# The first MLP matrix in seven block products instead of eight (Strassen), in a two-layer hybrid transformer step

## The reference

```python
def channel_mlp(x, shift, scale, gate, p):
    h = rms_norm(x, p['norm2']) * (1 + scale) + shift
    z = jax.nn.relu(h @ p['mlp_w1'])          # 1024 -> 4096
    return x + gate * ((z * z) @ p['mlp_w2'])  # 4096 -> 1024
```

## Time and profile before

| | |
|---|---|
| median of 3 runs | 1724.19 us (1720.06 to 1725.21) |
| profiled execution, its own time | 1722.82 us |
| its span in the profile | 1720.9 us |
| mean granted PE clock | 0.977 of 2.4 GHz |
| DMA | 160.14 MB, mean 93 GB/s |

### The profile page before, as it was taken

One profiled execution on the slowest core, in us unless ns is written; L12 is line 12 of the kernel. 1 busy time (PEld: TensorE's weight loads), 2 busy tenths in 40 slices (PEclk: granted clock), 3 DMA queues, 4 the chain that ended last, 5 costly groups with the idle time before them and its releaser, 6 DMA issues.

```text
span 1720.9 us, 28384 instructions
## 1 busy us (share of the span) xinstructions
PE 1599.7 (93%) x11714; PEld 1487.7 (86%) x11714; DVE 939.8 (55%) x1493; ACT 658.7 (38%) x1041; POOL 135.4 (8%) x99
## 2 busy tenths in 40 slices
PE   6878997899999999999987789888999999999998
PEld 4756894589999999999976569756999999999998
DVE  4554438846556554655565433596656545554553
ACT  4555434743322322233154463366443322332221
POOL 0003004400000000000000120253000000000000
PEclk9989998999999999999999899989999999999999
DMA  9620544212222222224534206441222222222311
GB/s 315 217 86 1 97 120 133 83 50 74 74 74 74 74 74 74 74 74 145 165 108 150 73 5 141 128 130 30 76 72 74 74 74 81 67 74 74 98 50 62
DMA packets 150855, 160.14 MB, mean 93 GB/s; under 512 B 16390, under 2 KB 132808, under 8 KB 150728
## 3 DMA queue, kind: packets, MB, share of 16 engines
q1 hardware_dynamic: 150024, 158.13, 30.3%
q10 hardware_dynamic: 576, 0.16, 0.0%
q0 software_dynamic: 128, 0.05, 0.0%
HBM read 153.41 MB, written 4.65 MB: 92 GB/s over the span
## 4 chain that ended last, share of the span: by engine, by line
PE 77%; DVE 10%; ACT 7%; issue 3%; SPq 1%; DMA 1%; ACTq 0%; DVEq 0%
PE ps L1591 33%; PE ps L1973 27%; PE ps L1730 10%; DVE extrema L1342 1%; PE ps L1754 1%; PE ps L1571 1%; ACT pt_c L783 1%; DVE extrema L1325 1%; PE ps L1807 1%; PE ps L1617 1%; SPq L606 1%; PE ps L1702 1%; PE ps L1785 1%; ACT pr_c L957 1%; DMA ada_room<-in_w_ada 1%
## 5 line engine op out<-in xcount | busy, mean ns | idle before, releaser
L1384 DVE SCALAR_TENSOR_TENSOR xT<-ps,mod,xT 128x128 f32<-128x128 f32 (+2 forms) x432 | 190.1, 440 | 198.0 <-PE ps L1591 186.1
L783 ACT ACTIVATE w_hi<-w_raw 128x2048 fp32r<-128x2048 f32 (+1 forms) x90 | 169.9, 1887 | 335.2 <-PE ps L1591 327.2
L1148 DVE TENSOR_TENSOR w_lo<-w_raw,w_hi 128x2048 fp32r<-128x2048 f32 (+1 forms) x90 | 203.1, 2257 | 142.6 <-ACT w_hi L783 141.2
L1973 PE MATMUL ps<-xa_hi,w_hi 128*128 128x320 f32 (+1 forms) x1024 | 236.2, 312 | 0.0
L1973 PE MATMUL ps<-xa_lo,w_hi 128*128 128x320 f32 (+1 forms) x1024 | 235.2, 311 | 0.0
L1973 PE MATMUL ps<-xa_hi,w_lo 128*128 128x320 f32 (+1 forms) x1024 | 235.2, 311 | 0.0
L1591 PE MATMUL ps<-z_hi,w_hi 128*128 128x320 f32 x1024 | 234.1, 310 | 0.9 <-DVE xT L1384 0.9
L1591 PE MATMUL ps<-z_lo,w_hi 128*128 128x320 f32 x1024 | 233.4, 309 | 0.0
L1591 PE MATMUL ps<-z_hi,w_lo 128*128 128x320 f32 x1024 | 233.3, 309 | 0.0
L1120 ACT ACTIVATE z_relu<-z_relu,sink_shift 128x128 f32<-128x128 f32 (+1 forms) x128 | 72.3, 564 | 307.4 <-DVE z_relu L1491 305.3
L1973 PEld LDWEIGHTS ps<-xa_hi,w_hi 128*128 128x128 f32 x1024 | 173.5, 189 | 0.3
(11 more groups left out here) (249 smaller groups left out, 2372.5 us busy)
## 6 DMA issues: line engine op xcount, KB each, us to landing
w_raw<-in_mlp_w SPq DMA_DIRECT2D x64, 1024.0 KB, 5.4
ada_own<-in_w_ada SPq DMA_DIRECT2D x54, 512.0 KB, 4.5
w_raw<-in_w_in SPq DMA_DIRECT2D x14, 1024.0 KB, 8.5
ada_mix<-in_w_ada SPq DMA_DIRECT2D x21, 512.0 KB, 7.6
ada_room<-in_w_ada SPq DMA_DIRECT2D x15, 512.0 KB, 9.7
w_raw<-in_w_out SPq DMA_DIRECT2D x8, 768.0 KB, 5.3
ada_first<-in_w_ada SPq DMA_DIRECT2D x6, 512.0 KB, 9.3
x_in<-in_x_sample SPq DMA_DIRECT2D x1, 2048.0 KB, 8.9
```

The source lines that it names most:

```text
L783: do(nc.scalar.activation(out, in_, ACT.Copy), sem)
L1148: do(V.tensor_tensor(w_lo[:, n % 2, 0:w], w_raw[:, n % 2, 0:w], f32(w_hi[:, n % 2, 0:w]), ALU.subtract), w_lo_ready)
L1384: do(V.scalar_tensor_tensor(dst, src, gate[:, m:m + 1], dst, ALU.mult, ALU.add), sem if last else None)
L1973: last = M.matmul(bank(b + a_, s1 - s0), w[r][:, k, c:c + P], x[:, k, s0:s1], start=k == 0 and q == 0, stop=k == KC - 1 and q == 2)
```

## The change

The w1 unit is now computed by Strassen's scheme. Its matrix is cut in two rows (hidden channels 0 to 127 and 128 to 255) by two columns (even and odd input chunks), and the input in even or odd chunks (b11 and b12, b21 and b22: first and second half of the tokens). Seven products of 4 k x 3 = 12 matmuls, each 322 columns wide, take the place of eight: 84 matmuls. Needed for that:

- Four sums of weight quarters, s1 to s4, per w1 unit (`sum_quarters`, DVE, 512 columns each), and four combinations of input halves, t1 to t4, made once a layer (`combine_halves`, DVE). The input now has seven parts of 4 x 322 columns, each with a hi half (ACT) and a lo half (DVE).
- Each w1 unit is split in seven blocks of 512 columns (11, s2, s1, s3, 12, 22, s4), each w2 unit in four; w_hi and w_lo are a ring of eight blocks. A block is split when the block eight places earlier has been multiplied.
- The products are put together from PSUM: two pairs of products add up in a bank (b11 x 11 stays in bank 0, is copied to `us[0]` by ACT, and 12 x b21 is added in the bank), the rest DVE adds in `take_u`, `take_22`, `take_11`, `take_21`, `take_12`.
- z is scaled in `z_raw`; ACT does relu in two segments, squares to z_hi and squares in place; DVE subtracts (`low_z`).
- The order of units alternates: w1, w1, w1, w2, w1, w2, ... (three w2 at the end).
- The adaLN loads of the next layer that went out before and after the last w1 unit all go out after it, since their places are now used by the MLP.

The diff, cut to its core:

```diff
         for g in range(GROUPS):
-            if g + 1 < GROUPS:
-                out += [(l, "w1", g + 1, j) for j in range(2)]
-            out += [(l, "w2", g, j) for j in range(2)]
+            for j in range(2):
+                out += [(l, "w1", g + 1, j)] * (g + 1 < GROUPS) + [(l, "w2", g, j)]
...
+W1_ORDER = ("11", "s2", "s1", "s3", "12", "22", "s4")
+W1_ORDER_FIRST = ("11", "22", "12", "s2", "s1", "s3", "s4")
+X_LO_ORDER = ("b11", "b21", "t4", "t2", "t1", "t3", "b22")
+XW = NTOK // 2 + 2
...
# SP
+                    sp.wait_ge(prod_done, 7 * W1_PER_LAYER * (l + 1))
+                    sp.wait_ge(u_read, 6 * W1_PER_LAYER * (l + 1))
+                    load_adas(48 * (l + 1), range(over + ROOM // 2))
                     load_adas(48 * (l + 1), range(over + ROOM // 2, over + ROOM))
...
# ACT, start of the MLP
+                for j in range(4):
+                    if j < 3:
+                        split_hi(U + 10 + j)
+                    else:
+                        for b in range(3):
+                            split_hi_block(first, b)
+                    for c in (2 * j, 2 * j + 1):
+                        act.wait_ge(m_dve, acc_ix.last_reader(acc_ix.at[(l, "wo", c)])[1])
+                        scale_halves(l, c)
+                        square_x(2 * l + 1, c)
+                        if c % 2 == 0 and c:
+                            round_halves(l, c // 2 - 1)
...
+                def square_z(n, row):
...
+                    act.wait_ge(z_scaled, 2 * w1_index(n) + (1 if row else 2))
+                    for m, s, e in SEGMENTS:
+                        do(nc.scalar.activation(z[:, s:e], z[:, s:e], ACT.Relu, bias=z_shift[:, row, m:m + 1],
+                                                scale=-1.0 if row else 1.0))
+                    do(nc.scalar.activation(z_hi[:, slot, :], z, ACT.Square))
+                    do(nc.scalar.activation(z, z, ACT.Square), z_squared)
...
+                    elif units[n][1] == "w1" and units[nxt][1] == "w2":
+                        split_hi_block(nxt, 0)
+                        copy_p1(n)
+                        for b in range(1, 4):
+                            split_hi_block(nxt, b)
+                        square_z(n, 1)
+                        square_z(n, 0)
...
# DVE, start of the MLP
+                    if d % 2 == 0 and d:
+                        combine_halves(l, d // 2 - 1)
+                    if d % 2 == 1 and d > 1:
+                        low_halves(l, d // 2 - 1)
+                sum_quarters(first, (1, 2))
+                combine_halves(l, 3)
+                low_halves(l, 3, X_LO_ORDER[0:4])
+                split_lo_blocks(first, (3,))
+                low_halves(l, 3, ("t1",))
+                split_lo_blocks(first, (4,))
+                low_halves(l, 3, ("t3",))
+                sum_quarters(first, (3, 4))
+                split_lo_blocks(first, (5,))
+                low_halves(l, 3, ("b22",))
+                split_lo_blocks(first, (6,))
                 mean(2 * l + 1)
...
+                def take_22(n):
...
+                    do(V.tensor_tensor(us[1][:, :], us[0][:, :], bank(3, HALF), ALU.add), u_read)
+                    do(V.tensor_copy(z_shift[:, 1, :], bank(2, XW)[:, HALF:XW]))
+                    do(V.tensor_tensor(z_raw[:, z_slot(n, 1), HALF:NTOK], us[1][:, :], bank(2, HALF), ALU.add), u_read)
...
+                take_u(first)
+                take_22(first)
+                take_11(first)
+                take_21(first)
+                take_12(first)
+                sum_quarters(first + 1, (1, 2))
+                split_lo_blocks(first + 1, (0, 1, 2))
+                sum_quarters(first + 1, (3, 4))
+                split_lo_blocks(first + 1, (3, 4, 5))
+                take_u(first + 1)
+                split_lo_blocks(first + 1, (6,))
                 invert(2 * l + 1)
+                scale_z(first, 1)
+                scale_z(first, 0)
+                low_z(first, 1)
+                take_22(first + 1)
+                sum_quarters(first + 2, (1, 2))
+                split_lo_blocks(first + 2, (0, 1))
+                take_11(first + 1)
+                low_z(first, 0)
+                sum_quarters(first + 2, (3, 4))
+                split_lo_blocks(first + 2, (2, 3, 4, 5))
+                take_21(first + 1)
+                scale_z(first + 1, 1)
+                split_lo_blocks(first + 2, (6,))
+                take_12(first + 1)
+                scale_z(first + 1, 0)
+                low_z(first + 1, 1)
+                low_z(first + 1, 0)
# DVE, all later units
+                    if units[n][1] == "w1":
+                        split_lo_blocks(nxt, (0,))
+                        take_u(n)
+                        split_lo_blocks(nxt, (1, 2))
+                        take_22(n)
+                        split_lo_blocks(nxt, (3,))
+                        take_11(n)
+                        if units[nxt + 1][1] == "w1":
+                            sum_quarters(nxt + 1, (1, 2))
+                        take_21(n)
+                        scale_z(n, 1)
+                        if units[nxt + 1][1] == "w1":
+                            sum_quarters(nxt + 1, (3, 4))
+                        take_12(n)
+                        scale_z(n, 0)
                     else:
+                        if units[n - 1][1] == "w1":
+                            low_z(n - 1, 1)
+                            low_z(n - 1, 0)
+                        for dd in range(4):
...
+                            elif units[nxt][1] == "w1":
+                                split_lo_blocks(nxt, ((0, 1), (2, 3), (4,), (5, 6))[dd])
...
+                            add_y(n, dd)
...
# PE
+                def products(n):
...
+                    pe.wait_ge(u_read, 6 * (i - 1) + 4)
+                    product(n, "11", "b11", 0)
+                    product(n, "s2", "t2", 1)
+                    pe.wait_ge(u_read, 6 * i)
+                    product(n, "s1", "t1", 2)
+                    product(n, "s3", "t3", 3)
+                    pe.wait_ge(u_read, 6 * i + 1)
+                    product(n, "12", "b21", 0, more=True)
+                    pe.wait_ge(u_read, 6 * i + 2)
+                    product(n, "22", "t4", 3, more=True)
+                    pe.wait_ge(u_read, 6 * i + 3)
+                    product(n, "s4", "b22", 2, more=True)
```

More of the change, by code:

```diff
@@ L1105, in _ @@
[L1105 to L1126 removed]
+                first = U + MLP0
@@ new lines, in _, with copy_p1 @@
+                for name in X_LO_ORDER:
+                    if name == "t4":
+                        act.wait_ge(x_combined, 4 * l + 4)
+                    copy(x_of("hi", name)[:, 3, :], x_of("raw", name)[:, 3, :], x_hi_ready)
+                    if name in ("t2", "t1", "t3"):
+                        split_hi_block(first, 3 + ("t2", "t1", "t3").index(name))
+                split_hi_block(first, 6)
+                def copy_p1(n):
+                    i = w1_index(n)
+                    act.wait_ge(prod_done, 7 * i + 1)
+                    if i:
+                        act.wait_ge(u_read, 6 * i)
+                    copy(us[0][:, :], bank(0, HALF), p1_copied)
@@ new lines, in take_21, with take_12 @@
+                def take_21(n):
+                    z = z_raw[:, z_slot(n, 1), :]
+                    b = 6 if n == first else 3
+                    dve.wait_ge(prod_done, 7 * w1_index(n) + 6)
+                    do(V.tensor_tensor(z_shift[:, 1, :], z_shift[:, 1, :], bank(b, XW)[:, HALF:XW], ALU.add))
+                    do(V.tensor_tensor(z[:, 0:HALF], us[1 if n == first else 0][:, :], bank(b, HALF), ALU.add), u_read)
+                def take_12(n):
+                    z = z_raw[:, z_slot(n, 0), HALF:NTOK]
+                    dve.wait_ge(prod_done, 7 * w1_index(n) + 7)
+                    do(V.tensor_tensor(z, us[0][:, :], bank(2, HALF), ALU.add), u_read)
@@ new lines, in add_y @@
+                def add_y(n, dd):
+                    u = units[n]
+                    d = 4 * u[3] + dd
+                    if u[2] == GROUPS - 1 and l + 1 < DEPTH:
+                        for c in {5: (1, 2), 6: (3, 4), 7: (5, 6)}.get(d, ()):
+                            add_square(2 * (l + 1), c)
+                    dve.wait_ge(y_done, (l * GROUPS + u[2]) * KC + d + 1)
+                    b = 4 + 2 * (d % 2)
+                    v = ps[:, 512 * b:512 * b + 1024].rearrange("p (a n) -> p a n", a=2)[:, :, 0:HALF]
+                    add_gated(d, mod[:, l % 2, GATE2 + d, :], v, y_read)
@@ L1953, in _, with product @@
                 begin_acc((l, "sum2"))
-                for n in range(13, 45):
-                    u = units[U + n]
-                    s = (U + n) % 2
+                first = U + MLP0
+                def product(n, block_name, x_name, b, ks=range(4), more=False):
+                    order = w1_order(n)
+                    i = order.index(block_name)
+                    pe.wait_ge(w_lo_ready, splits(n, i))
+                    w = [ring_block(x, n, i) for x in (w_hi, w_lo)]
```

(8 more changed lines are left out.)

391 lines of the change are left out of this document (244 added, 147 removed).

## The result

The changed kernel takes **1856.76 us** (median of four runs, 1854.10 to 1858.82) where the kernel before takes 1724.19: a ratio of **1.0773**, 95% interval 1.0751 to 1.0795. The forecast was 1808, range 1750 to 1832. The direction and the waits are those of the forecast; the size needs one thing more, the mechanism of a rival that had 6%, "The clock falls too", at 1856.

A forecast was written before the change was run, and what follows sets the result against it. PE was taken to bound the kernel, 100% busy in the MLP. 54.4 us less matmul time plus 2 x (40.6 + 28.4) us of stalls turned 1722.8 into 1806.4, 1808 as median; range 1750 to 1832.

The forecast's parts named there:

- The clock falls too: Rival, 6%: PE's clock falls at each of the 28 stalls, 1.75 us per fall, 49 us more, 1856 us.
- What it removes from PE: w1 units: 84 matmuls for 96, 12.56 us against 14.26, 54.4 us less over 32 units.
- What it adds elsewhere: DVE and ACT in the MLP: 23.5 us of DVE work per pair against 26.6 of PE, fits as a sum.
- DVE busy near 80% of a pair: Sign that the forecast is right: DVE's busy share in a pair of w1 and w2 units.
- Short chained instructions pack closer: Rival, 3%: 17 DVE instructions before add_y's end each 0.1 us shorter, stall 1.3 us, time 1763 us.
- One steady pair: w1 plus w2 unit: PE stalls 2.9 us before column 2, pair 29.56 us for 28.34; 40.6 us of waits a layer.
- The start of each MLP: First three w1 units: PE stalls of 6.8, 3.1, 7.3 us and the third unit's wait, 28.4 us a layer.
- The sum: Whole kernel: 1722.8 - 54.4 + 2 x (40.6 + 28.4) = 1806.4 us, 1808 as median.
- the forecast case: Whole kernel: steady and start stalls both come, 1808 us, own range 1794 to 1832; given 76%.
- the one wait of this kind: End of layer 0, before the change: PE waits 0.90 us for DVE's add; cited against a clock fall.
- At nothing: w_out stage and moved adaLN loads: PE covers DVE's 12.7 us with 14.1, w2 units cover the loads; no cost.

The follow-up runs named there:

- e2: Changed kernel with DVE's add_y of column 0 moved ahead of low_z of row 0, later add_y ahead of their weight blocks: 1726.15 us, ratio 1.0002.
- e3: Changed kernel with only the next unit's weight blocks moved behind each add_y, both low_z staying ahead of the first: 1775.02 us, ratio 1.0274.
- e5: e2 without the second norm's reciprocal, one DVE operation per layer, so z is multiplied by the root: 1716.06 us, ratio 0.9952.
- e8: e2 with the second norm's root and reciprocal taken on five columns and spread over 640 columns by PE: 1718.73 us, ratio 0.9963.
- e1: Changed kernel with 18 dummy matmuls in PE's wait for column 2's bank in w2 units: 1810.95 us, ratio 1.0489.
- e7: e2 with 27 dummy fp32 matmuls per layer in the two long waits of the MLP's start: 1725.43 us, ratio 1.0007.
- e4: e2 with the four block sums of each w1 unit on POOL instead of DVE: 1720.72 us, ratio 0.9965.

## Why the prediction was right, and where it was wrong

**What it removes from PE**: right. A unit's 84 matmuls take 12.50 us undisturbed (e2; forecast 12.56), a w2 unit 14.07 (14.08). A w1 unit is 14.26 - 12.50 = 1.76 us shorter, 56 us for 32 of them, for 54.4; twelve matmuls in one bank cost nothing, as the earlier trace rows said.

**What it adds elsewhere**: right to 0.1 us over a chain of 17 DVE instructions; a 320-column addition takes 0.49 plus 0.03. The sign "DVE busy near 80% of a pair" reads 71% (22.04 of 31.18 us), since its 23.5 us counted the gaps between instructions as work and the pair came out longer. The rival "Short chained instructions pack closer" falls with it, and so does, for this kernel, the overhead of some 60 ns in the Trainium skill's Perfetto Trace Analysis, section Optimizing Scalar/DVE Operations: each chained instruction shows its full duration and the gap of the earlier trace rows.

**One steady pair**: the wait is right (2.80 for 2.9, in the place named, ended by DVE xT), its cost was not. The forecast priced it at its idle time alone. Measured, a wait of this length costs 2.80 + 0.26 + 1.54 = 4.60 us.

**The start of each MLP**: right in sum, 78.75 for 79.2, not in its parts. The waits of layer 0 come to 19.6 us, for 28.4, because the matmuls behind them run at the low clock and fill some of the time in which DVE is late anyway. In e2 the stretch is 67.55, less 2.15 for the sums of squares and 37.5 for three units: 27.9 us more than PE's work at full clock, of which 22.45 are idle (67.55 - 45.10) and the rest is low clock and restarts.

**The sum**: the term that failed is the clock's, put at zero in the forecast case. The rival "The clock falls too" had it, 28 x 1.75 = 49 us and 1856. Measured are 26 falls and 43.8 us: 1.54 us at most of them, down to 1.27 where part of the low clock lies in the wait, and 2.73 to 2.79 in the four longer pairs (10.09 us for 48 matmuls instead of 8.84). That the rival's 1856 meets 1856.76 is luck: its falls are some 5 us too dear, and it has neither the restarts, 28 x 0.26 = 7.3 us, nor the 6.7 us outside the MLP, nor the steady waits that came out 4 us shorter in all (38.6 and 38.3 us a layer for 40.6). The step that failed is the sentence that spoke against it: "at the one wait of this kind, 0.90 us at 864.83, it stayed at 2.4 GHz". That wait was a third as long as the one I had just worked out, and I took it for the same kind. Nor did the rows show that short waits are safe: the fall in w_out, from which the price of 1.75 us was taken, starts 0.3 us after PE has come out of two waits of 0.91 and 0.87 us, at 357.29 and 359.04. The profiles of all ten kernels have these two waits ahead of w_out in both layers; w_out takes 52.8 us in 12 of the 20 places and 51.3 in the other 8, so one fall there costs 1.53. Of the two other rows, 10 us stretches at 0.52 and 1.00, neither has one wait in the middle of full work. The rows told of waits of 0.9 us, with both outcomes, and for 2.9 they bore out neither answer: the chance should have been near one half, and the case's own range, 1794 to 1832, should have reached to 1856.

The Trainium skill's TensorE: Matmul & The Clock Gate, section HAM oscillation, describes the effect that I had set aside, waits that put the matmuls behind them back to the low clock. Its case is another one, short bursts with a wait after each; here one wait stands in some 28 us of full work. The trace after agrees as far as that the clock is low behind all 26 steady waits of 2.78 to 3.32 us; behind the waits of 1.35 us in e3 it stays at 1.00.

**At nothing**: w_out stays covered (PE busy 51.29 of 51.29 us), and no wait on adaLN weights shows in the MLP.

What stays open: what sets the moment of the fall, and with it the four longer pairs, and why the start's wait of 2.92 us brings a fall in some executions only; no run varied that. The unchanged code's 6.7 us are not explained either; profiled executions of the later kernels have w_out end anywhere from 408.2 to 415.1 us, so part of it may be a difference between executions. A start with the second unit's takes moved ahead of the first unit's scale_z was not tried: z_shift is one buffer, and they would write it before ACT has read it for the first unit.

## What to carry to other kernels

When a change puts waits into an unbroken stretch of matmuls, price each beyond its idle time (here 1.35 us cost 1.6, 2.80 us cost 4.6), and look for a row with a wait as long as the one you forecast; a shorter one is no evidence. Where PE waits for an engine that has time to spare, move what PE waits for ahead of work that isn't due (e2: some 130 us for a few lines moved); where that engine is truly short, as in the start, only work taken from it helps (e5, e8).

## What the runs showed of the hardware

- The clock falls to 0.50 with a single wait in the middle of full work: at all 26 waits of 2.78 to 3.32 us and both of 2.21 us; not at 1.63, 1.50 or 1.35 us. It goes down between 0.8 us before the restart and 1.1 us after it, at a cost of 1.27 to 1.55 us, or 2.8 in the four places where it stays low twice as long. Between 1.63 and 2.21 us steady pairs have no wait.
- In the start, where one wait follows another, length alone doesn't tell: behind the same 2.92 us the clock fell in 5 of 12 places, and behind 0.91 and 0.87 us it fell in 12 of 20.
- A restart costs 0.26 us at full clock beyond the idle time shown: 48 matmuls in 7.30 us behind waits of 1.35 us (e3) and behind filled ones (e1), 7.04 in a row.
- Dummy matmuls in a wait keep the clock (e1, e7), and are worth it only where PE's rate sets what comes next.
- DVE is slower beside POOL: with POOL adding 512 columns (1.54 us), DVE's instruction on two SBUF operands at 640 columns took 1.12 us for 0.83, at 320 columns 0.77 for 0.49, while one that reads PSUM stayed at 0.49 (e4 against e2). Whether POOL is slowed too, no run shows.
